# Differential attention in a two-layer kernel: one fp32 copy of turned queries and keys, low parts on GpSimd, and another order and grouping of each attention step

## The reference

```
qd = rms_norm(q_d.reshape(B, S, 8, 2, 64), g_q);  kd = rms_norm(k_d..., g_k)
for each block i of 128 queries (4 of them), keys 0 .. 128*(i+1):
    s = einsum(qb, kb) * 64**-0.5 - slope[h] * dist,  causal      # two score maps j per head
    p = softmax(s);   a = p[:, :, 0] - lam * p[:, :, 1]
    out_i = einsum(a, v)
```

## Time and profile before

| what | value |
|---|---|
| median of 3 runs | 991.08 us (989.12 to 992.71) |
| profiled execution | 994.6 us, its span 992.8 us (1.8 us lie around the span) |
| TensorE busy | 955.5 us, 96% of the span |
| VectorE, ScalarE, GpSimd busy | 417.8, 406.2, 472.8 us |
| chain that ended last | PE 85%, DVE 6%, ACT 3%, POOL 3%, issue 2%, DMA 1% |
| granted TensorE clock | 0.993 on average; 1.00 in the attention's stretch |
| HBM traffic | 78.71 MB in DMA packets, mean 79 GB/s |

### The profile page before, as it was taken

One profiled execution on the slowest core, in us unless ns is written; L12 is line 12 of the kernel. 1 busy time (PEld: TensorE's weight loads), 2 busy tenths in 40 slices (PEclk: granted clock), 3 DMA queues, 4 the chain that ended last, 5 costly groups with the idle time before them and its releaser, 6 DMA issues.

```text
span 992.8 us, 13091 instructions
## 1 busy us (share of the span) xinstructions
PE 955.5 (96%) x4792; PEld 771.9 (78%) x4792; DVE 417.8 (42%) x998; ACT 406.2 (41%) x892; POOL 472.8 (48%) x448
## 2 busy tenths in 40 slices
PE   6999999999999999999999999999999989899998
PEld 5878888876888877777777877888788867677777
DVE  3200139034114433765655433226556665465431
ACT  5333242334224344455455422346344354465531
POOL 3443445524446744664344444424567737633342
PEclk9999999999999999999999999999999979999999
DMA  6322211322333322222212242222324411100013
GB/s 215 107 86 85 85 43 43 107 64 87 104 96 96 87 83 85 65 64 65 65 42 65 91 164 65 84 83 82 107 71 119 119 53 41 52 6 21 23 43 106
DMA packets 41167, 78.71 MB, mean 79 GB/s; under 512 B 3296, under 2 KB 5088, under 8 KB 41104
## 3 DMA queue, kind: packets, MB, share of 16 engines
q1 hardware_dynamic: 40240, 76.30, 25.7%
q10 hardware_dynamic: 864, 1.57, 0.5%
HBM read 75.74 MB, written 2.12 MB: 78 GB/s over the span
## 4 chain that ended last, share of the span: by engine, by line
PE 85%; DVE 6%; ACT 3%; POOL 3%; issue 2%; DMA 1%; SPq 0%; ACTq 0%; DVEq 0%; POOLq 0%
PE Z L1577 23%; PE Z L1579 22%; PE Z L1578 22%; PE A L1802 4%; PE A L1810 2%; PE A L1704 2%; PE A L1717 2%; PE A L1587 2%; PE A L1577 1%; PE A L1770 1%; PE A L1579 1%; PE A L1578 1%; POOL w_lo L811 1%; PE A L1730 1%; PE Z L1661 1%
## 5 line engine op out<-in xcount | busy, mean ns | idle before, releaser
L811 POOL TENSOR_TENSOR w_lo<-raw,w_hi 128x512 fp32r<-128x512 f32 (+1 forms) x262 | 341.6, 1311 | 424.2 <-ACT w_hi L521 423.2
L1577 PE MATMUL Z<-w_hi,hT_hi 128*128 128x512 f32 (+1 forms) x832 | 339.6, 408 | 8.7 <-POOL w_lo L811 2.7
L1579 PE MATMUL Z<-w_hi,hT_lo 128*128 128x512 f32 (+1 forms) x832 | 324.8, 390 | 0.0
L1578 PE MATMUL Z<-w_lo,hT_hi 128*128 128x512 f32 (+1 forms) x832 | 324.3, 390 | 0.0
L521 ACT CAST w_hi<-raw 128x512 fp32r<-128x512 f32 (+1 forms) x262 | 157.9, 614 | 278.7 <-PE Z L1579 256.9
L1577 PEld LDWEIGHTS Z<-w_hi,hT_hi 128*128 128x128 f32 x832 | 156.8, 189 | 52.9 <-issue 9.0
L1579 PEld LDWEIGHTS Z<-w_hi,hT_lo 128*128 128x128 f32 x832 | 156.7, 188 | 33.1
L1578 PEld LDWEIGHTS Z<-w_lo,hT_hi 128*128 128x128 f32 x832 | 157.3, 189 | 26.7
L1577 PE MATMUL Z<-w_hi,oT_hi 128*128 128x512 f32 x128 | 51.6, 403 | 3.3 <-DVE tmp L1109 2.2
L637 ACT ACTIVATE x_sb<-x_sb,nmax 128x128 f32<-128x128 f32 (+3 forms) x64 | 35.5, 557 | 38.3 <-DVE nmax L1264 38.3
L1579 PE MATMUL Z<-w_hi,oT_lo 128*128 128x512 f32 x128 | 50.0, 391 | 0.0
(11 more groups left out here) (220 smaller groups left out, 1386.8 us busy)
## 6 DMA issues: line engine op xcount, KB each, us to landing
raw<-in_w_in SPq DMA_DIRECT2D x92, 512.0 KB, 3.7
raw<-in_w_out SPq DMA_DIRECT2D x16, 512.0 KB, 3.7
raw<-in_ret_w_o SPq DMA_DIRECT2D x8, 512.0 KB, 3.3
raw<-in_diff_w_o SPq DMA_DIRECT2D x8, 512.0 KB, 3.4
x_sb<-in_x SPq DMA_DIRECT2D x8, 256.0 KB, 5.5
x_sb<-in_x SPq DMA_DIRECT2D x4, 512.0 KB, 6.6
out<-x_sb SPq DMA_DIRECT2D x8, 256.0 KB, 3.2
raw<-in_w_in SPq DMA_DIRECT2D x4, 416.0 KB, 3.2
```

The source lines that it names most:

```text
L811: pool.tensor_tensor(w_lo[:, s % SPLIT_SLOTS, 0:width], raw[:, c % RAW_SLOTS, s - CHUNK_START[c], 0:width], w_hi[:, s % SPLIT_SLOTS, 0:wid ...
L1577: pe.matmul(out, l_hi, r_hi, start=first, stop=False)
L1578: pe.matmul(out, l_hi, r_lo, start=False, stop=False)
L1579: return pe.matmul(out, l_lo, r_hi, start=False, stop=last)
```

## The change

1. ACT copies the turned queries or keys once, with their gain, out of `A[2]` into a new fp32 buffer `qk_f` in SBUF, then copies from there into `qT_hi` or `kT_hi`. The bank is free after the first copy (`qk_out`).
2. POOL makes the low parts: `qk_f` minus the high part, both from SBUF. DVE's `diff_queries` and `diff_keys` go.
3. `diff_turn` moves from i = 1, 2 to i = 0, 1, into part B, and loses its own yield; a head takes 8 yields instead of 10, 72 in all instead of 86, and `diff_due` is scaled to it: 27, 46 and 72 where 36, 58 and 86 stood.
4. On PE `scores(n+1)` moves from part B to the head of part A, in front of `turn_probs(n-2)` and `outputs(n-3)`.

```diff
@@ -109,10 +109,10 @@
     if v < DIFF_FIRST:
         return 0
     if v < DIFF_SECOND:
-        return 36 * (v - DIFF_FIRST + 1) // (DIFF_SECOND - DIFF_FIRST)
+        return 27 * (v - DIFF_FIRST + 1) // (DIFF_SECOND - DIFF_FIRST)
     if v < DIFF_THIRD:
-        return 36 + 22 * (v - DIFF_SECOND + 1) // (DIFF_THIRD - DIFF_SECOND)
-    return min(86, 58 + 28 * (v - DIFF_THIRD + 1) // (DIFF_LAST - DIFF_THIRD))
+        return 27 + 19 * (v - DIFF_SECOND + 1) // (DIFF_THIRD - DIFF_SECOND)
+    return min(72, 46 + 26 * (v - DIFF_THIRD + 1) // (DIFF_LAST - DIFF_THIRD))
 
 
 ATT_STEPS, ATT_WAIT, ATT_SLOTS = 71, 6, 58
...
@@ -257,6 +257,8 @@
         with ExitStack() as scope:
             q2_hi = sb("q2_hi", [P, 2, S], F32R, scope)
             q2_lo = sb("q2_lo", [P, 2, S], F32R, scope)
+        with ExitStack() as scope:
+            qk_f = sb("qk_f", [P, 2, S], F32, scope)
         v_hi = sb("v_hi", [P, TT * 256], F32R)
         v_lo = sb("v_lo", [P, TT * 256], F32R)
         bias = sb("bias", [P, 2, S], F32)
...
@@ -615,15 +617,14 @@
                         if hh == 0 and p + 1 < pairs:
                             turned_q(p + 1)
 
-            def diff_queries(w):
-                act.wait_ge(qk_t, 2 * w + 1)
-                act.activation(qT_hi[:, w % 2, :], diff_qk_bank(w, 0)[:, :], ACT.Copy,
-                               scale=gains(DIFF, w)[0]).then_inc(qk_hi, 1)
-
-            def diff_keys(w):
-                act.wait_ge(qk_t, 2 * w + 2)
-                act.activation(kT_hi[:, w % 2, :], diff_qk_bank(w, 1)[:, :], ACT.Copy,
-                               scale=gains(DIFF, w)[1]).then_inc(qk_hi, 1)
+            def diff_qk(w, i):
+                act.wait_ge(qk_t, 2 * w + i + 1)
+                if w:
+                    act.wait_ge(qk_lo, 2 * w + i - 1)
+                act.activation(qk_f[:, i, :], diff_qk_bank(w, i)[:, :], ACT.Copy,
+                               scale=gains(DIFF, w)[i]).then_inc(qk_out, 1)
+                act.wait_ge(qk_out, 2 * w + i + 1)
+                act.copy((qT_hi, kT_hi)[i][:, w % 2, :], qk_f[:, i, :]).then_inc(qk_hi, 1)
 
             def diff():
 
...
@@ -637,9 +638,8 @@
                             act.activation(p, p, ACT.Exp, bias=nmax[:, j, n:n + 1], scale=-1.0,
                                            accum_out=rsum[:, n, j:j + 1]).then_inc(s_exp, 1)
                     yield
-                    if i in (1, 2) and h + 1 < H:
-                        (diff_queries if i == 1 else diff_keys)(h + 1)
-                        yield
+                    if i in (0, 1) and h + 1 < H:
+                        diff_qk(h + 1, i)
                     if i == 2 and n >= 6:
                         hd = (n - 6) // 4
                         act.wait_ge(o_mm, 4 * hd + 4)
...
@@ -902,6 +902,11 @@
                 pool.tensor_scalar(bias[:, h % 2, :], dist[:, :], 2.0 ** -h, 0.5, ALU.mult,
                                    ALU.mult).then_inc(bias_r, 1)
 
+            def diff_qk(w, i):
+                pool.wait_ge(qk_hi, 2 * w + i + 1)
+                hi_, lo_ = ((qT_hi, qT_lo), (kT_hi, kT_lo))[i]
+                pool.tensor_tensor(lo_[:, w % 2, :], qk_f[:, i, :], hi_[:, w % 2, :], ALU.subtract).then_inc(qk_lo, 1)
+
             def diff():
 
                 N = 4 * H
...
@@ -1234,16 +1241,6 @@
                         head_sums(p - 2)
                 head_sums(pairs - 1)
                 scale_heads()
-
-            def diff_queries(w):
-                dve.wait_ge(qk_hi, 2 * w + 1)
-                dve.scalar_tensor_tensor(qT_lo[:, w % 2, :], diff_qk_bank(w, 0)[:, :], gains(DIFF, w)[0],
-                                         qT_hi[:, w % 2, :], ALU.mult, ALU.subtract).then_inc(qk_lo, 1)
-
-            def diff_keys(w):
-                dve.wait_ge(qk_hi, 2 * w + 2)
-                dve.scalar_tensor_tensor(kT_lo[:, w % 2, :], diff_qk_bank(w, 1)[:, :], gains(DIFF, w)[1],
-                                         kT_hi[:, w % 2, :], ALU.mult, ALU.subtract).then_inc(qk_lo, 1)
 
             def diff():
 
...
@@ -1286,16 +1283,10 @@
                         dve.scalar_tensor_tensor(p0, p0, rinv[:, m, 0:1], prob_at(DIFF, 1, m, wm), ALU.mult,
                                                  ALU.add).then_inc(s_comb, 1)
                     yield
-                    if i in (1, 2) and h + 1 < H:
-                        (diff_queries if i == 1 else diff_keys)(h + 1)
-                        yield
                     yield
 
             def diff_slot(g, k, steps, norms):
                 v = TT * (KD * (g - G_DIFF0) + k)
-                if g == G_DIFF0 and k == 1:
-                    diff_queries(0)
-                    diff_keys(0)
                 for t in range(TT):
                     if normed_in(g) and 2 <= TT * k + t <= 8 and t % 2 == 0:
                         head_sums(2 * k + t // 2 - 1, squares_d)
...
@@ -1679,8 +1670,10 @@
             def diff_turn(w, i):
 
                 c0 = q_cols(DIFF, w)[i]
-                if 4 * w - 4 + i > 0:
-                    pe.wait_ge(p_lo, 4 * w - 4 + i)
+                if w:
+                    pe.wait_ge(qk_out, 2 * w + i)
+                if 4 * w - 5 + i > 0:
+                    pe.wait_ge(p_lo, 4 * w - 5 + i)
                 if w == H // 2:
                     pe.wait_ge(head_normed, 12 + 4 * i)
                 for t in range(TT):
...
@@ -1723,8 +1716,8 @@
                     if m:
                         pe.wait_ge(p_lo, m)
                     job, mi = divmod(m + 1, 4)
-                    if mi in (1, 2) and job + 1 < H:
-                        pe.wait_ge(qk_lo, 2 * job + 2 + mi)
+                    if mi in (0, 1) and job + 1 < H:
+                        pe.wait_ge(qk_out, 2 * job + 3 + mi)
                     for kb in range(m % 4 + 1):
                         kk = slice(P * kb, P * (kb + 1))
                         last = pe.transpose(A[2][:, kk], prob_at(DIFF, 0, m, S)[:, kk], ident[:, :])
...
@@ -1734,16 +1727,15 @@
                 scores(0)
                 for n in range(N + 4):
                     h, i = divmod(n, 4)
+                    if n + 1 < N:
+                        scores(n + 1)
                     if 0 <= n - LAG < N:
                         turn_probs(n - LAG)
                     if 0 <= n - 3 < N and i != 3:
                         outputs(n - 3)
                     yield
-                    if i in (1, 2) and h + 1 < H:
-                        diff_turn(h + 1, i - 1)
-                        yield
-                    if n + 1 < N:
-                        scores(n + 1)
+                    if i in (0, 1) and h + 1 < H:
+                        diff_turn(h + 1, i)
                     if 0 <= n - 3 < N and i == 3:
                         outputs(n - 3)
                     yield
```

More of the change, by code:

```diff
@@ L321, in build @@
         p_by_act, p_by_dve = sem("p_by_act"), sem("p_by_dve")
-        k_roped, k_cat = sem("k_roped"), sem("k_cat")
+        k_roped, k_cat, qk_out = sem("k_roped"), sem("k_cat"), sem("qk_out")
         p_t, p_hi, p_lo, o_mm, o_out = sem("p_t"), sem("p_hi"), sem("p_lo"), sem("o_mm"), sem("o_out")
@@ L710, in diff_slot @@
                 if g == G_DIFF0 and k == 1:
-                    diff_queries(0)
-                    diff_keys(0)
+                    diff_qk(0, 0)
+                    diff_qk(0, 1)
                 if g + 1 in EARLY and k >= 4:
```

## The result

The changed kernel takes 1028.66 us (median of 4 runs, 1026.79 to 1029.14) where the kernel before takes 991.89 us in the same comparison (4 runs, 989.12 to 993.11): a ratio of 1.037, 95% interval 1.0349 to 1.0392. It is slower, as forecast, but by 36.8 us instead of 20, and outside the range of 997 to 1020. Its profiled execution took 1028.96 us.

The account below looks back on a forecast made before the run. PE was taken to bound the stretch, busy 206.8 of 210.3 us. New score waits of 23.2 us less 3.5 of old idle gave net +20: 991.1 + 20 = 1011 us, range 997 to 1020.

Parts of the forecast that it names:

- A(n): First part of attention step n, where PE now asks for reduce n; before, it asked half a step later.
- n = 0: First step, scores(0) and scores(1) together: two reduces with their signals are bare, PE waits 0.9 us.
- A(2): First part of step 2, v = 29: the gate take of v = 28 stands ahead, wait 2.0 us.
- A(7), A(11): Steps 7 and 11, start of groups 15 and 16: DVE stands behind head_sums, wait 3.85 us, twice.
- A(22): First part of step 22, v = 157: a take behind ACT's key copies and a w_hi, wait 2.7 us.
- Rival (a): Faster: DVE has reduced before PE reaches the scores, the idle goes; 986 us, chance 0.10.
- Sum: ... = 23.2 ... Net +20: Attention stretch: forecast score waits total 23.2 us, less the old 3.5 us of idle, net +20.
- A(9): First part of step 9, v = 84: eight norm pieces stand ahead, wait 3.0 us (1.1 to 4.8).
- A(13): First part of step 13, v = 115: seven norm pieces stand ahead, wait 2.9 us (1.1 to 4.8).
- A(21): First part of step 21, v = 153: five 16-column norm pieces ahead, one perhaps stretched, wait 1.7 us.
- rival (c): Larger loss: the 16 GpSimd subtractions stretch DVE's operations again; +27 to +33 us, 1021, chance 0.11.
- A(27): First part of step 27, among the other steps: DVE needs 2.1 to 2.4 us, PE comes later, no wait.

Follow-up runs that it names:

- order_alone: The kernel before with only scores(n+1) moved to the head of part A; 1022.38 us, ratio 1.0316.
- maxima_early: The changed kernel with DVE's maxima of scores n+1 made one step ahead, in its step n; 995.32 us, ratio 1.0044.
- no_norm_pieces: The changed kernel without the 16 norm pieces of groups 15 and 16, part of the computation left out; 1016.14 us, ratio 1.0239.
- no_head_sums: The changed kernel without POOL's squares and DVE's sums in groups 15 and 16, part of the computation left out; 1014.61 us, ratio 1.0234.
- gap_long: The kernel before with PE held up at eight places, each for six chained ACT copies; 1044.99 us, ratio 1.0541.
- gap_short: The kernel before with PE held up at eight places, each for two chained ACT copies; 1005.24 us, ratio 1.0147.
- low_parts_alone: The kernel before with only the fp32 copy on ACT and the low parts on GpSimd; 992.33 us, ratio 1.0007.
- order_undone: The changed kernel with scores(n+1) put back into part B, behind the turn of queries or keys; 1001.37 us, ratio 1.0107.
- turns_one_step_later: The kernel of order_undone with the turns of queries and keys back at i = 1 and 2; 998.55 us, ratio 1.007.

## Why the prediction was half right

**Mechanism and places: right.** PE asks in A(n) for what stands at the same place in DVE's in-order list, and reduce n brings DVE's other work with it. All nine forecast places are there and their sizes at n = 0, A(2), A(7), A(11) and A(22) hold within 0.3 us. order_alone and maxima_early show the mechanism from both sides, no_norm_pieces and no_head_sums show whose work is exposed where. Rival (a) is out: DVE was never ahead at these places.

**The step that failed: the sum.** "Sum: ... = 23.2 ... Net +20" has no term for TensorE's clock. The prediction read 1.00 from the earlier trace rows and kept it, though its own schedule put eight waits of 1.7 to 3.9 us into a PE that had been busy 98% of the time. "No matmul's start-to-start changed" fell with it: 0.43 instead of the 0.23 of the earlier trace rows behind the waits. The missing term measured 12.7 us in the changed kernel; gap_long and gap_short show that it follows from the waits alone (18.0 us of busy time for eight long ones, 2.3 for eight short ones). The other term that was too small is the waiting itself, 28.9 us where 23.2 was forecast.

**A second, smaller mis-size: waits behind short operations.** A(9), A(13) and A(21) took 12.1 us instead of 7.6, which is 4.5 of the 5.7; the first two lie within the high ends that the text gave. DVE's and POOL's timelines of the changed kernel at A(9):

```profile
421.99 0.17 DVE L1077 TENSOR_SCALAR rs_a<-stat 128x32 f32<-128x32 f32 x1
...
425.10 0.19 DVE L1035 TENSOR_TENSOR rs_b<-rstd 128x32 f32<-128x32 f32 x1
425.28 1.30 POOL L908 TENSOR_TENSOR qT_lo<-qk_f,qT_hi 128x512 fp32r<-128x512 f32 x1 [0.49 <-ACT qT_hi L627]
425.32 1.30 DVE L1036 SCALAR_TENSOR_TENSOR rs_b<-rs_b,rs_a 128x32 f32<-128x32 f32 x1
...
430.32 0.40 DVE L1261 CUSTOM_DVE_ANT_0 x_sb<-A,bias 128x256 f32<-128x256 f32 x1
```

The pieces took from 421.99 to 430.25, 8.3 us where 7.0 was taken. It is the picture of the earlier trace rows once more. One of the stretched operations stands beside the new subtraction `qT_lo`: 1.30 us instead of 0.19, ending as it ends. The prediction weighed ahead what the Trainium skill, SBUF — State Buffer, section "Who interferes with whom", says of this: a DVE operation with two inputs in SBUF and a GpSimd one that reads SBUF exclude each other. By that rule the trace agrees. At A(13) the same pair stands at 466.92 (DVE, 1.27 us) and 466.88 (`qT_lo`). At A(21) two operations are stretched, and the text had reckoned with one at most:

```profile
514.32 1.27 POOL L908 TENSOR_TENSOR qT_lo<-qk_f,qT_hi 128x512 fp32r<-128x512 f32 x1 [2.64 <-ACT qT_hi L627]
514.48 1.15 DVE L1036 SCALAR_TENSOR_TENSOR rs_b<-rs_b,rs_a 128x16 f32<-128x16 f32 x1
515.55 1.26 POOL L811 TENSOR_TENSOR w_lo<-raw,w_hi 128x512 fp32r<-128x512 f32 x1
515.66 1.19 DVE L1037 SCALAR_TENSOR_TENSOR rstd<-rs_b,rstd 128x16 f32<-128x16 f32 x1
```

So rival (c)'s mechanism exists, about 1.1 us beside `qT_lo` at each of these three places, as an estimate up to 3.3 of the 4.5 us; it was not tried alone in the new order. It did not cause the larger loss; low_parts_alone shows that where the half step hides reduce n it costs nothing.

**A(27): "in all other steps ... no wait" failed** by 1.19 us. POOL's and DVE's timelines:

```profile
553.11 1.28 POOL L908 TENSOR_TENSOR kT_lo<-qk_f,kT_hi 128x512 fp32r<-128x512 f32 x1 [2.24 <-ACT kT_hi L627]
...
554.35 1.29 POOL L811 TENSOR_TENSOR w_lo<-raw,w_hi 128x512 fp32r<-128x512 f32 x1
...
555.63 0.55 POOL L919 TENSOR_SCALAR x_sb<-x_sb,rinv,lam 128x256 f32<-128x256 f32 x1
...
556.22 0.82 DVE L1283 SCALAR_TENSOR_TENSOR x_sb<-x_sb,rinv 128x256 f32<-128x256 f32 x1 [2.25 <-POOL x_sb L919]
```

The new subtraction pushes POOL's `w_lo` and with it the scaling of map 1; DVE's combination waits 2.25 us for that, and reduce 27 stands behind it in DVE's list. This is read from one timeline and was not tried alone.

**Priced at nothing, and right:** merging PE's parts (at most 0.4 us by maxima_early), 12 us less of DVE work and the earlier release of the bank (both in low_parts_alone, ratio 1.0007). Over the PE work of the earlier trace rows (338.90 to 588.30 us) DVE, ACT and POOL are busy 101, 113 and 120 us, where 100, 112 and 122 were forecast. (the earlier trace rows is not groups 13 to 19 exactly: its window begins 7 us before v = 4 and ends 3.5 us before v = 208. The idle time of 3.5 us is the same in both cuts.) **The old idle time** went as forecast, all but 0.9 of 3.5 us.

**What stays open.** order_undone and turns_one_step_later keep 10 and 8 us. Their profiles show 9.1 and 8.8 us of waits, nearly all at other places (the take at v = 33, turns at 88, 118 and 155), and 3.2 us more PE busy time each, with some 3 us of missing clock. These two together are the 8.8 and 8.4 us by which the stretch is longer than before. That these come from 72 yields falling elsewhere than 86 is the explanation left over; no run changes the number of yields alone.

## What to carry to other kernels

When a wait is moved earlier in one engine's list, look up where its releaser stands in the other engine's in-order list, and add up all that stands between the two: each of the eight waits of 1.8 us and more here came from some other piece of work in front of a pair of reduces of 0.4 to 1.2 us. If the consumer moves ahead by half a step, move the producer with it, which brought back 33 of 37 us here. And price a wait of about 4 us on TensorE at some 1.5 times its length, since the matmuls behind it run at the lower clock: the stretch grew by 50.6 us for 32.6 of idle in gap_long, by 27.3 for 18.5 in order_alone, by 39.1 for 26.4 in the changed kernel. Eight waits of 1.5 us cost 1.2 times their length, and between 1.8 and 3 us either can happen (next section).

## What the runs showed of the hardware

The length of the wait alone doesn't tell whether the clock falls. It stayed at 1.00 in gap_short behind eight waits of up to 2.1 us, and fell in the changed kernel behind 1.93 (v = 29) and 1.78 (v = 161; it ends 8 us after the one before). The same wait can go either way: the one at v = 29 (1.92 or 1.93 us) has the clock down behind it in the changed kernel and in no_head_sums and not in no_norm_pieces; the one of 2.97 us at v = 157 does the same. Counted over this stretch in all twelve profiles, the clock fell behind each of the 22 waits of 3.6 us and more and behind 11 of the 19 from 1.78 to 3.0. It may also fall late: in gap_long it was still 1.00 in the first microsecond after PE went on, and 0.53 in the next two.

The lower level also turns up where the change isn't. Outside the stretch the kernel before was granted less than 1.00 in places where the changed one was not. Windows of the kernel before:

```profile
710.00:720.00 10.00, 8.23 (x34) 6.58 (x33) 2.75 (x4) 3.42 (x7) 5.59 (x5) 0.83 0.18 52
...
810.00:820.00 10.00, 9.32 (x39) 7.52 (x40) 7.88 (x27) 4.20 (x11) 2.80 (x4) 0.67 0.19 55
```

With the window between them at 800 to 810 us (0.84) that is 6.6 us of missing clock, and the windows 36 us later in the changed kernel show 1.00. Nor does this hang on the change. The span less the stretch is 781.0 to 781.6 us in five of the twelve profiles (the changed kernel, maxima_early, gap_short, no_norm_pieces, no_head_sums) and 784.7 to 786.1 in the other seven (before, gap_long and order_alone among them), which have the clock down in at least two windows of 10 us there (the five in one at most); gap_short and gap_long differ from before only inside the stretch and fall on either side. It answers to the 4.7 us by which the changed kernel's profile is shorter outside the stretch, and to the gap of 2.7 us between the profiled execution of before and its median: the sum of a forecast made against one profiled execution carries such chance with it.
